# Adding the experts' results to the tokens by one-hot products instead of a scatter and a reload

## The reference, cut to what matters

```python
def hier_moe(x, w_group, w_expert, w_gate, w_up, w_down):
    ...
    weight = g_w * e_w / jnp.sum(e_w, -1, keepdims=True)
    expert = (g_idx * M_PER_GROUP + e_idx).reshape(-1)
    ...
    xs = xt[tok_sorted]
    hid = jax.nn.silu(lax.ragged_dot(xs, w_gate, sizes)) * lax.ragged_dot(xs, w_up, sizes)
    ys = lax.ragged_dot(hid, w_down, sizes) * weight.reshape(-1)[order][:, None].astype(x.dtype)
    return jax.ops.segment_sum(ys, tok_sorted, num_segments=n_tok).reshape(b, s, d)
```

## Time and profile before

| | |
|---|---|
| median of 3 runs | 2706.35 us |
| span of the profiled execution | 2704.4 us |
| PE busy (matmul) | 2507.2 us, 93% |
| PE weight loads (beside it) | 1852.0 us, 68% |
| DVE busy | 1077.4 us, 40% |
| ACT busy | 754.9 us, 28% |
| POOL busy | 182.2 us, 7% |
| DMA | 576.56 MB, mean 213 GB/s |

### The profile page before, as it was taken

One profiled execution on the slowest core, in us unless ns is written; L12 is line 12 of the kernel. 1 busy time (PEld: TensorE's weight loads), 2 busy tenths in 40 slices (PEclk: granted clock), 3 DMA queues, 4 the chain that ended last, 5 costly groups with the idle time before them and its releaser, 6 DMA issues.

```text
span 2704.4 us, 36859 instructions
## 1 busy us (share of the span) xinstructions
PE 2507.2 (93%) x14582; PEld 1852.0 (68%) x14582; DVE 1077.4 (40%) x1628; ACT 754.9 (28%) x1221; POOL 182.2 (7%) x302
## 2 busy tenths in 40 slices
PE   8997999788899979998788899999999999999999
PEld 7675665444576656664454677888888877888887
DVE  4753110100345641110001666656642666556542
ACT  3530000000245410000001353543332454434331
POOL 0001111111000001111111000000000010000000
PEclk9998999999999989999999999999999999999999
DMA  6339999999722189999998422222332312223231
GB/s 172 85 145 382 405 406 409 411 408 406 267 94 79 40 329 405 405 405 411 408 407 334 170 67 90 79 94 94 100 134 93 102 48 95 85 92 103 94 125 55
DMA packets 175401, 576.56 MB, mean 213 GB/s; under 512 B 20560, under 2 KB 104080, under 8 KB 125618
## 3 DMA queue, kind: packets, MB, share of 16 engines
q1 hardware_dynamic: 164722, 558.07, 54.5%
q0 software_dynamic: 10560, 16.81, 1.9%
HBM read 569.56 MB, written 23.07 MB: 219 GB/s over the span
## 4 chain that ended last, share of the span: by engine, by line
PE 68%; SPq 20%; DMA 5%; DVE 3%; issue 3%; ACT 2%; DVEq 0%; POOLq 0%; POOL 0%; ACTq 0%
PE ps L232 16%; PE ps L234 16%; PE ps L233 16%; SPq L1175 13%; SPq L1181 7%; PE ps L1325 6%; PE ps L1343 4%; DMA r_x<-resid 1%; DMA first_ring<-in_moe_w_gate 1%; PE ps L1295 1%; DMA first_weights<-in_moe_w_up 1%; ACT lat_probs L1833 1%; PE ps L1642 1%; PE ps L2330 1%; PE ps L1658 1%
## 5 line engine op out<-in xcount | busy, mean ns | idle before, releaser
L1325 PE MATMUL ps<-first_weights,moe_xsT 128*64 128x256 f32 x2688 | 311.3, 381 | 46.4 <-DMA first_weights<-in_moe_w_up 27.6
L232 PE MATMUL ps<-l_h_hi,l_w_hi 128*128 128x512 f32 x896 | 353.0, 394 | 0.0
L233 PE MATMUL ps<-l_h_lo,l_w_hi 128*128 128x512 f32 x896 | 348.8, 389 | 0.0
L234 PE MATMUL ps<-l_h_hi,l_w_lo 128*128 128x512 f32 x896 | 348.8, 389 | 0.0
L1404 DVE TENSOR_TENSOR moe_hid<-moe_silu,ps 128x256 f32<-128x256 f32 x64 | 27.0, 422 | 783.8 <-PE ps L1325 783.8
L1325 PEld LDWEIGHTS ps<-first_weights,moe_xsT 128*64 128x64 f32 x2688 | 223.9, 137 | 143.6 <-issue 93.7
L2882 DVE TENSOR_TENSOR l_w_lo<-l_raw,l_w_hi 128x2048 fp32r<-128x2048 f32 x76 | 174.1, 2293 | 270.2 <-ACT l_w_hi L2627 270.2
L1377 ACT ACTIVATE moe_ys<-ps 128x512 f32<-128x512 f32 x64 | 38.2, 597 | 678.9 <-PE ps L1343 678.9
L1343 PE MATMUL ps<-first_weights,moe_hidT 128*64 128x512 f32 x672 | 172.1, 658 | 38.3 <-DVE moe_hidT L1406 38.3
L2627 ACT ACTIVATE l_w_hi<-l_raw 128x2048 fp32r<-128x2048 f32 x76 | 145.6, 1918 | 179.4 <-PE ps L234 168.5
L232 PEld LDWEIGHTS ps<-l_h_hi,l_w_hi 128*128 128x128 f32 x896 | 168.3, 188 | 37.4 <-issue 2.9
(11 more groups left out here) (589 smaller groups left out, 4351.3 us busy)
## 6 DMA issues: line engine op xcount, KB each, us to landing
first_weights<-in_moe_w_up SPq DMA_DIRECT2D x84, 1024.0 KB
first_weights<-in_moe_w_down SPq DMA_DIRECT2D x84, 1024.0 KB
first_weights<-in_moe_w_gate SPq DMA_DIRECT2D x84, 1024.0 KB
first_ring<-in_moe_w_up SPq DMA_DIRECT2D x44, 1024.0 KB
first_ring<-in_moe_w_down SPq DMA_DIRECT2D x44, 1024.0 KB
l_raw<-in_ffn_up SPq DMA_DIRECT2D x44, 1024.0 KB, 5.1
first_ring<-in_moe_w_gate SPq DMA_DIRECT2D x40, 1024.0 KB
l_raw<-in_w_in SPq DMA_DIRECT2D x22, 1024.0 KB, 5.2
```

Source lines behind the costliest of these rows:

```text
L232: pe.matmul(out, stationary[0], moving[0], start=first, stop=False)
L233: pe.matmul(out, stationary[0], moving[1], start=False, stop=False)
L234: return pe.matmul(out, stationary[1], moving[0], start=False, stop=last)
L1325: ins = pe.matmul(k.ps[64 * h:64 * h + 64, 2 + m, 0:256], xsT[:, j, :], piece[:, j % 4, 256 * h:256 * h + 256], start=j == 0, stop=j == ND ...
```

## The change

The results of a block stay on chip. Four things change.

- **Combine.** For each block a 128x512 selection matrix `sel` says which of the 512 tokens the slot of each row holds (a comparison of the tokens' numbers with the slot's token). ACT copies the down products as a rounded high part `ys_hi`, DVE makes the rest as a low part `ys_lo`, both fp32r. While PE works on the next block, it multiplies `sel` with both: `combine(b, t)` adds, for tile t of 128 tokens, four products of 512 columns over 64 rows each, one after each of the first three quarters of the gate and up products and one after the turning of the hidden values. DVE then adds the tile's 128x1024 sums out of PSUM to the tokens, which stand in SBUF multiplied by ALPHA. The slot's weight is multiplied in with the up products.
- **No scatter, no reload.** `y_dram`, the scatters and their waits on POOL, ACT and SP, the reload of 4 MB, the identity and diagonal products are gone. `Opening.add` adds the last block's sums for tiles 2 and 3 at the start of the next stage. The next stage's first weights go to a buffer of their own (`raw`) and their low parts come after the first two tiles' norms.
- **Routing** makes the slot's token and weight in place of `r.put`; the weights as three bf16 parts that products sum, later than `r.put` was made.
- **POOL** copies a block's token numbers and weights to `slot` ahead of the gather, after DVE's previous selection.

The diff, cut:

```diff
         pe.wait_ge(self.laid, 1)
-        for a in range(8):
-            ins = pe.matmul(k.ps[0:SLOTS, 3, 0:2 * COLS], self.in_slot[:, a, :], self.in_blk[:, a, 0:2, :].rearrange("p a b -> p (a b)"), start=a == 0, stop=a == 7)
-        ins.then_inc(self.listed, 1)
+        for h in range(2):
+            for a in range(8):
+                ins = pe.matmul(k.ps[SLOTS * h:SLOTS * h + SLOTS, 3, 0:2 * COLS], self.in_slot[:, a, :], self.in_blk[:, a, 0:2, :].rearrange("p a b -> p (a b)"),
+                                start=a == 0, stop=a == 7)
+            ins.then_inc(self.listed, 1)
+        k.run_on(pe, 3)
         pe.wait_ge(self.laid, 2)
         for h in range(2):
             for a in range(8):
-                ins = pe.matmul(k.ps[SLOTS * h:SLOTS * h + SLOTS, 7, 0:2 * COLS], self.in_slot[:, a, :], self.in_blk[:, a, 2:4, :].rearrange("p a b -> p (a b)"),
+                ins = pe.matmul(k.ps[SLOTS * h:SLOTS * h + SLOTS, 7, 0:3 * COLS], self.in_slot[:, a, :], self.in_blk[:, a, 1:4, :].rearrange("p a b -> p (a b)"),
                                 start=a == 0, stop=a == 7)
         ins.then_inc(self.listed, 1)
-        k.run_on(pe, 3)
...
-    def add(self, k, pe, t):
-
-        pe.wait_ge(self.spread, self.norm + 1)
-        pe.wait_ge(self.y_in[t], 16 * (self.norm + 1))
-        for half in range(2):
-            for c in range(TOPK):
-                ins = pe.matmul(k.ps[:, 2 * t + half, :], self.diag[:, c, t, :], self.rows[t][:, c, half * 512:(half + 1) * 512], start=False, stop=c == TOPK - 1)
-        ins.then_inc(self.collected, 1)
+    def add(self, k, dve, t):
+
+        n, row = 2 * self.norm + t - 1, k.resid[:, t, :].rearrange("p (h c) -> p h c", h=2)
+        dve.wait_ge(self.summed, n)
+        dve.tensor_tensor(row, row, k.ps[:, 2 * t:2 * t + 2, :], ALU.add).then_inc(self.added, 1)
+        dve.wait_ge(self.added, n)
...
+            sp.wait_ge(used[WEIGHT_SETS - 1][5], TURNS)
             for m in range(2):
                 src, j = early(m)
-                sp.dma_start(k.early[:, m, :].rearrange("p (j c) -> p j c", j=j), src).then_inc(r.early_in, 16)
-            wait_then_tick(sp, ys_out, n * 16 + (EXPERTS - 1) * 16, tick_sp)
-            wait_then_tick(sp, xsT_kept, n + EXPERTS, tick_sp)
-            cl.load(sp, 0)
-            cl.load(sp, 1)
+                sp.dma_start(cl.raw[:, m, :].rearrange("p (j c) -> p j c", j=j), src).then_inc(r.early_in, 16)
             cl.load_gains(k, sp)
-            cl.load(sp, 2)
-            cl.load(sp, 3)
...
+                wait_then_tick(pool, sel_made, b + 1, tick_pool)
+                pool.tensor_copy(slot[:, :, :], r.slots[:, :, bass.ds(b, 1)]).then_inc(slot_set, 1)
                 wait_then_tick(pool, rows_turned, b + 2, tick_pool)
                 gather(b + 2)
 
-                wait_then_tick(pool, ys_out, b * 16, tick_pool)
-                pool.tensor_copy(put[:, :], r.put[:, bass.ds(b, 1)]).then_inc(put_set, 1)
-                wait_then_tick(pool, put_set, b + 1, tick_pool)
-                wait_then_tick(pool, ys_kept, b + 2, tick_pool)
-                pool.indirect_dma_start(out=r.y_dram, out_offset=bass.IndirectOffsetOnAxis(ap=put[:, 0:1], axis=0),
-                                        in_=ys[:, :], in_offset=None, bounds_check=SEQ * TOPK * 2 - 1, oob_is_err=False).then_inc(ys_out, 16)
-
...
+            def gate_up(s, times, c, ahead):
+
+                out, piece = (gate_out, up_out)[c // 2], piece_in(s, times, c, ahead)
+                for i in range(4):
+                    j = 4 * (c % 2) + i
+                    for h in range(2):
+                        ins = pe.matmul(out(slice(64 * h, 64 * h + 64)), xsT[:, j, :], piece[:, i, 256 * h:256 * h + 256], start=j == 0, stop=j == ND - 1)
+                ins.then_inc(used[s][c], 1)
+
+            def combine(b, t, last=False):
+
+                if t == 0:
+                    wait_then_tick(pe, sel_made, b + 2, tick_pe)
+                    wait_then_tick(pe, ys_low, b + 2, tick_pe)
+                if t >= 2 or later(b):
+                    wait_then_tick(pe, added, 4 * b + t - 1, tick_pe)
+                for part in (ys_hi, ys_lo):
+                    for h in range(2):
+                        rows_ = slice(64 * h, 64 * h + 64)
+                        ins = pe.matmul(sums(t)[:, h, :], sel[rows_, t * P:(t + 1) * P], part[rows_, :], start=part is ys_hi, stop=part is ys_lo)
+                ins.then_inc(cl.summed if last and t >= 2 else combined, 1)
 
             def body(s, times, b, ahead=False):
+                before = [lambda t=t: combine(b - 1, t) for t in range(NT)] if later(b) else [lambda: None] * NT
                 wait_then_tick(pe, xsT_kept, b + 1, tick_pe)
 
...
+                for c in range(4):
+                    gate_up(s, times, c, ahead)
+                    if c < 3:
+                        before[c]()
...
                 ins.then_inc(hid_turned, 1)
+                before[3]()
                 wait_then_tick(pe, hidT_kept, b + 1, tick_pe)
-                wait_then_tick(pe, ys_kept, b + 1, tick_pe)
+                wait_then_tick(pe, ys_low, b + 1, tick_pe)
...
-            blocks = n + (EXPERTS - 1)
-            pe.wait_ge(grown, NT)
-            wait_then_tick(pe, xsT_kept, blocks + 1, tick_pe)
-            wait_then_tick(pe, hidT_kept, blocks, tick_pe)
-            for t in range(2):
-                own(k, pe, t)
-            wait_then_tick(pe, ys_kept, blocks + 1, tick_pe)
-            own(k, pe, 2)
-            own(k, pe, 3)
+            for t in range(NT):
+                combine(n + (EXPERTS - 2), t, last=True)
...
-                act.wait_ge(ys_out, b * 16)
+                act.activation(silu[:, :], gate_out(every), ACT.Silu).then_inc(silued, 1)
                 act.wait_ge(used[s][5], times + 1)
-                act.activation(ys[:, :], k.ps[:, 4, :], ACT.Copy).then_inc(ys_kept, 1)
+                act.activation(ys_hi[:, :], k.ps[:, DOWN, :], ACT.Copy).then_inc(ys_kept, 1)
...
+            def add(b, t):
+                row = k.resid[:, t, :].rearrange("p (h c) -> p h c", h=2)
+                dve.wait_ge(combined, 4 * b + t + 1)
+                dve.tensor_tensor(row, row, sums(t), ALU.add).then_inc(added, 1)
+
             def body(s, times, b):
+                behind = not (isinstance(b, int) and b == 0)
+                if behind:
+                    for t in range(3):
+                        add(b - 1, t)
                 dve.wait_ge(silued, b + 1)
...
-                dve.tensor_tensor(hid[:, :], silu[:, :], k.ps[:, 3, 0:256], ALU.mult).then_inc(hid_kept, 1)
+                dve.wait_ge(slot_set, b + 1)
+                dve.scalar_tensor_tensor(hid[:, :], silu[:, :], slot[:, 0, :], up_out(every), ALU.mult, ALU.mult).then_inc(hid_kept, 1)
...
-                dve.tensor_copy(xsT[:, :, :], k.ps[:, 0, :].rearrange("p (j s) -> p j s", j=ND)).then_inc(xsT_kept, 1)
-
-            for_each_block(dve, n, body)
-            dve.wait_ge(first_hi, 1)
-            dve.tensor_tensor(cl.split[0][1][:, :], k.early[:, 0, :], cl.split[0][0][:, :].bitcast(F32), ALU.subtract).then_inc(first_lo, 1)
-            dve.wait_ge(first_lo, 1)
+                dve.tensor_copy(xsT[:, :, :], k.ps[:, TURN, :].rearrange("p (j s) -> p j s", j=ND)).then_inc(xsT_kept, 1)
+                if behind:
+                    add(b - 1, 3)
+                dve.tensor_scalar(sel[:, :], iota[:, :], slot[:, 1, :], None, ALU.is_equal).then_inc(sel_made, 1)
+                dve.wait_ge(ys_kept, b + 1)
+                dve.tensor_tensor(ys_lo[:, :], k.ps[:, DOWN, :], ys_hi[:, :].bitcast(F32), ALU.subtract).then_inc(ys_low, 1)
+
+            for s in range(WEIGHT_SETS):
+                body(s, 0, s)
+            for_each_block(dve, n, body, 1)
+            for t in range(2):
+                add(n + (EXPERTS - 2), t)
...
             def stats(t):
-                dve.wait_ge(cl.collected, t + 1)
-                cm.stats_of_sum(k, dve, t)
+                if t >= 2:
+                    cl.add(k, dve, t)
+                cm.stats_of_rows(k, dve, t)
...
-            dve.sem_inc(lo_made, 1)
-            low(1)
             stats(0)
-            cm.centre(k, dve, 0, tile_banks(0))
+            cm.centre(k, dve, 0)
             cm.finish(k, dve, 0)
             stats(1)
-            cm.centre(k, dve, 1, tile_banks(1))
+            cm.centre(k, dve, 1)
             cm.finish(k, dve, 1)
             split_low(0)
+            low(0)
             split_low(1)
+            low(1)
             stats(2)
-            cm.centre(k, dve, 2, tile_banks(2))
+            cm.centre(k, dve, 2)
             cm.finish(k, dve, 2)
```

More of the change, by code:

```diff
@@ L177, in __init__ @@
         self.ps = nc.alloc_psum_tensor("ps", [P, 8, 512], F32)
-        self.y_in = [nc.alloc_semaphore(f"y_in{t}") for t in range(NT)]
-        self.gain_in, self.spread = nc.alloc_semaphore("gain_in"), nc.alloc_semaphore("spread")
+        self.gain_in, self.summed, self.added = (nc.alloc_semaphore(n) for n in ("gain_in", "summed", "added"))
```

(19 more changed lines are left out.)

190 lines of the change are left out of this document (84 added, 106 removed).

## The result

The changed kernel takes 2734.93 us (median; 2732.63 us the fastest) against a median of 2704.94 us before in the same rounds: 1.0107 times the time before, 95% interval 1.0093 to 1.0121. One of its four runs took 4307.45 us at a mean granted clock of 0.554 and stands outside this ratio. The profiled execution took 2735.55 us, its span is 2733.7 us, 29.3 us more than the 2704.4 us before.

A forecast was written before the change was run, and what follows sets the result against it. PE, at 15.6 us a block, was taken to bound both expert stages: 19.6 + 17.8 + 1 - 4 - 1 = +33 us, giving a 2737.8 us span and 2740 us as a run; range 2690 to 2790.

The forecast's parts named there:

- PE becomes the bound throughout: Both expert stages: PE sets the pace from first block to last, 15.6 us a block, and weights are never waited for.
- One sign that I had named: Changed profile, expert stages: the DMA share should be under 1, where it had been 1.02.
- A group at 0.8 us: Each of three exposed groups among the gate and up products costs PE 0.8 us, 2.4 us a block.
- rival (a): PE in the expert stages: pairs do not overlap, 17.0 us a block, 87 us more, 2827 us; chance 0.05.
- Rival (c): PE's groups: each second pair loads its weights in the open, 0.11 us each, 20 more, 2760 us; chance 0.08.
- The fourth group hidden: Behind the turning of hidden values: the group fits PE's 0.91 us wait for DVE; uncovered, another 0.8 us.
- The wait for the low part: Ahead of a block's first group: PE's queue works off a wait and an address, 0.1 to 0.3 us, taken as 0.2.
- The full clock: PE's block base: 13.0 us at full clock, not 13.58, as the fourth group fills the wait preceding the lower clock.
- rival (b): PE in the expert stages: the lower clock stays in one block of three, 35 us more, 2775 us; chance 0.12.
- DMA time freed, nothing bought: Expert stages: the scatter's 2.45% of DMA engine time is freed but buys nothing, since PE sets the pace.
- the faster case: Expert stages: a group under 0.6 us with its wait leaves weights setting the pace, 2679 us; chance 0.18.
- The ends: Outside the expert stages: first routing +1 us, second 0, stretch between the stages -4, behind the second stage -1.

The follow-up runs named there:

- the merged groups: Changed kernel with tiles 0 and 1's products together after the second quarter, tiles 2 and 3's after the turned hidden values: 2680.71 us, 0.9916 of before.
- the two runs without and with that group: Changed kernel with the combine left out for all blocks but the last: 2683.18 us; the same but keeping tile 3's fourth group: 2681.97 us.
- the one with added products: Kernel with the merged groups plus sixteen products on constants in PE's idle places of the first opening: 2680.5 us, 0.991 of before.
- two waits moved: Changed kernel with the waits for the low part and first weight piece put ahead of the fourth group: 2712.42 us, 1.0034 of before.

## Why the prediction was right

- **PE becomes the bound throughout.** Forecast: 15.6 us a block from first to last. Measured 15.53, even from first to last, and the kernel without the low parts shows that PE's products, and not weights or DVE, make it. One sign that I had named did not come: the DMA share stayed at 1.00 and 1.02, as in the earlier trace rows. My own sum, 15.9 us of transfers for a block of 15.6, spoke against that sign.
- **A group at 0.8 us.** Measured 0.81. The parts I put together were 0.46 for the products, 0.10 for entering, 0.21 within; measured 0.46, 0.11 in each of the four quarters, and 0.20 within (0.66 less 0.46). Pairs run at once: in the merged groups fp32r pairs of 512 columns follow each other 0.23 us apart, as single whole-array products do, so rival (a) falls. What the fixed part of the earlier trace rows is made of, a bare load and an emptying, was my estimate; the runs show its size, not its parts. Rival (c) had every second pair start 0.11 us late. In a group of its own it does (0.34 us after the first, for 0.23), but that is part of the 0.20 that I had counted once; merged, the third and fourth pair follow at the bare 0.23. The delay belongs to the place, not to each second pair.
- **The fourth group hidden.** Yes: 1.42 us against 1.41.
- **The wait for the low part.** Forecast 0.2 us, measured 0.1. The 0.1 us of signalling ahead of the low part was an estimate too: in the block shown with the result DVE starts it at 259.39 us, 0.02 after ACT's copy (258.77 and 0.60 long). Blocks of the first turns, written out without a loop, take 15.44 us and have no such wait (13.0 and 2.44 make it), blocks in the loop mostly 15.55. This is the step that was mis-sized: 0.1 less for the wait, against 0.04 more for the three groups, makes 62 steps of 15.53 in place of 15.6, 4.1 us less, and the whole miss is 3.7 (29.3 for 33 in the span).
- **The full clock.** I took 13.0 and not 13.58 as the base, because the fourth group fills the wait behind which the clock fell. Shown by the two runs without and with that group; rival (b) falls.
- **DMA time freed, nothing bought.** Shown: the write put back costs 0.06 us a block. The floor that I gave for the faster case, 2679 us, was 2683 us in the kernel without the combine. The faster rival needed a group under 0.6 us with its wait; groups merged by twos get there.
- **DVE.** Additions of 1.22 us for the 1.23 taken; the third ends ahead of the hidden values and nothing waits for it.
- **The ends.** Routing: +1 forecast, -0.2 measured; the first rows are turned at 225.94 us, before at 226.12. But the wait ahead of it is another: before, it ended with the gather, now PE's row there says `[2.32 <-PEq L604]`, which is PE's own queue behind the products for the weights. In the change and the experiments, whose code up to there is the same, this turning starts at 225.94 to 228.80 us, so one execution can't tell the +1. The stretch between the stages: -4 forecast and -4.1 measured, but not for my reasons alone: that the two agree is luck. The opening gave 1.5 us of it (39.7 after the last down product for 41.2, where I had 36.8; the terms that I gave add to 36.3, since 5.1 and 1.1 are 6.2 and not 6.5), the rest came later, but for the second routing in code that the change leaves as it was. And this stretch is not steady: in the kernels above whose code there is the change's own (all but the one with added products) it took 298.4 us (two waits moved) to 304.6 us (low parts left out), and the opening in it from 37 to 40 us, as the place varies in which the clock rises again. One profiled execution cannot tell 4 us there. My term left the clock out: with the identity and diagonal products gone, PE idles and is granted 0.63 and 0.67 of the full clock in the 20 us from 731 on, where before it had 1.00 from 725 on. Where the clock was back at 1.00 ahead of the last turning, the opening took 37.0 to 37.7 us, near my 36.8. Behind the second stage DVE's last norm ends 41.9 us after the down products (41.5 forecast, 42.4 before), but the program's end came 0.3 us later and not 1 sooner. That stretch, from the last turning of the hidden values on, took 1227.9 to 1229.3 us in the change and the experiments and 1228.8 before, so this term can't be told from its scatter. The routing's 1.2 us less and this end's 1.3 us more cancel, which is luck too.

## What to carry to other kernels

Work that is moved from one resource to another must be priced against what the new resource has left in that very stage: PE had 2.0 us to spare in a block and got 2.5 us, and the transfers freed were worth nothing until PE was under the weights' pace again. Where small products of another shape are interleaved, count the places and not the products: a place costs its changes of shape (here 0.35 us), and the pairs in it followed each other 0.23 us apart, so two places of eight beat four places of four by 1.1 us a block: 0.7 for the two places less, 0.3 because the third group went where PE's queue idled (0.14 us for 0.46 of products), 0.1 for the wait for the low part. And put waits that are long satisfied ahead of products that can cover them, not between the products and the one that matters: here that was 0.30 us a block.

## What I had not expected of the hardware

Two wait instructions that held PE for nothing cost it 0.30 us a block (15.53 to 15.23) between the fourth group and the down products, and nothing ahead of that group. A wait of 0.9 us behind the turnings was enough to bring the granted clock down in a third of the blocks, with down products of 5.3 us in place of 3.65, and four products of 512 columns in that wait prevented it in all. And the low clock in the opening, down to 0.53 over 10 us, cost nothing measurable as long as DVE was the longer chain; where it came again ahead of the last turning, it cost 1.5 to 2.7 us.
